# First layer of a two-layer expert lookup: u and v rows gathered as pairs, dense u and v tiles loaded as pairs

## What is computed

```python
u = jnp.take(u_tab, eid, axis=0)
act = jax.nn.gelu(jnp.einsum('chkd,cd->chk', u, hc)) * gate
v = jnp.take(v_tab, eid, axis=0)
return jnp.einsum('chk,chkd->cd', act, v)
```

## Time and profile before

| | us |
|---|---|
| runs (3): lowest, median, highest | 4078.24, 4083.88, 4086.14 |
| the profiled execution | 4085.21 |
| its span, from the first to the last instruction | 4083.4 |
| its stage with dense tiles, about | 815 to 1835 |

### The profile page before, as it was taken

The page is one execution under the profiler, slowest core; times in us unless marked ns, Lnnn a source line. Parts: engine busy times, 40 slices in busy tenths (PEclk is TensorE's granted clock), DMA queues, the critical chain, the costliest instruction groups (busy, mean ns, idle before and its releaser), DMA issues. The chain is left out here.

```text
span 4083.4 us, 41719 instructions
## 1 busy us (share of the span) xinstructions
PE 3591.4 (88%) x14914; PEld 2631.6 (64%) x14914; DVE 2362.9 (58%) x4846; ACT 649.1 (16%) x1760; POOL 889.4 (22%) x776
## 2 busy tenths in 40 slices
PE   7989987798888999988997776655999999999999
PEld 3678875687777777776784322222777676777676
DVE  2654778977788767776548887776352401352400
ACT  2531111400000000005212111101001301001300
POOL 0000000165565555540004444442000000000000
PEclk9999997999999999999999888776999999999999
DMA  4466545799999999982668999997883345683343
GB/s 173 152 178 195 148 140 204 233 392 409 409 408 369 409 409 409 408 339 90 175 186 337 417 421 383 423 422 318 277 300 112 134 155 166 222 306 114 134 155 113
DMA packets 523735, 1096.67 MB, mean 269 GB/s; under 512 B 25844, under 2 KB 339188, under 8 KB 489494
## 3 DMA queue, kind: packets, MB, share of 16 engines
q1 hardware_dynamic: 408824, 554.12, 40.0%
q0 software_dynamic: 110592, 536.92, 32.6%
q10 hardware_dynamic: 4128, 3.15, 0.3%
HBM read 1078.36 MB, written 15.73 MB: 268 GB/s over the span
## 5 line engine op out<-in xcount | busy, mean ns | idle before, releaser
L2556 PE MATMUL ps<-hT,wring 128*128 128x256 f32 x2560 | 559.7, 379 | 1.7 <-DMA wring<-in_ffn_w_up 1.7
L1676 PE MATMUL ps<-hT,wring 128*128 128x256 f32 x2048 | 485.1, 391 | 81.8 <-DVE hT L1836 79.3
L2556 PEld LDWEIGHTS ps<-hT,wring 128*128 128x128 f32 x2560 | 485.8, 190 | 85.3 <-issue 13.1
L1676 PEld LDWEIGHTS ps<-hT,wring 128*128 128x128 f32 x2048 | 388.4, 194 | 174.0 <-DVE hT L1836 120.3
L1710 POOL DMA_INDIRECT gu<-in_u_tab,eid x256 | 285.5, 1115 | 948.1 <-POOLq L134 621.4
L1667 PE MATMUL ps<-hT,wring 128*128 128x256 f32 x2048 | 464.9, 380 | 1.1 <-ACT G L1749 1.1
L1667 PEld LDWEIGHTS ps<-hT,wring 128*128 128x128 f32 x2048 | 390.5, 191 | 54.5 <-issue 1.1
L2032 PE MATMUL ps<-pairs,diag 128*128 128x512 f32 x520 | 290.2, 719 | 134.0 <-ACT diag L2127 134.0
L1860 DVE SCALAR_TENSOR_TENSOR wring<-gv,wgt,wring 128x1024 f32<-128x1024 f32 x254 | 326.6, 1286 | 109.1 <-DMA gv<-in_v_tab,eid 97.2
L1843 DVE CUSTOM_DVE_ANT_0 gu<-gu,htok 128x1024 f32<-128x1024 f32 x256 | 313.2, 1224 | 121.8 <-DMA gu<-in_u_tab,eid 116.2
L1716 POOL DMA_INDIRECT gv<-in_v_tab,eid x256 | 290.6, 1135 | 220.3 <-DVE wring L1860 154.7
(11 more groups left out here) (385 smaller groups left out, 4561.8 us busy)
## 6 DMA issues: line engine op xcount, KB each, us to landing
wring<-in_u_first SPq DMA_DIRECT2D x128, 512.0 KB
wring<-in_v_tab SPq DMA_DIRECT2D x128, 512.0 KB
room<-in_ada_w SPq DMA_DIRECT2D x32, 1536.0 KB, 11.5
wring<-in_ffn_w_gate SPq DMA_DIRECT2D x44, 1024.0 KB, 8.9
wring<-in_ffn_w_up SPq DMA_DIRECT2D x44, 1024.0 KB, 11.4
wring<-in_ffn_w_down SPq DMA_DIRECT2D x44, 1024.0 KB, 5.0
wring<-in_w_in SPq DMA_DIRECT2D x72, 512.0 KB, 6.6
wring<-in_w_mod SPq DMA_DIRECT2D x28, 1024.0 KB, 5.6
```

The costliest lines, as they stand in the source:

```text
L1676: m = nc.tensor.matmul(ps[:, n // 2, (n % 2) * S:(n % 2 + 1) * S], vslot[:, e % 2, n * P:(n + 1) * P], act_[:, e % 3, :], start=e == 0 and ...
L2556: m = mm(ps[:, b + n, q * S:(q + 1) * S], up_slot(s, q)[:, k, n * P:(n + 1) * P], hT[:, k, 0:S], start=k == 0, stop=k == KD - 1)
```

## The change

The u and v tables are laid out side by side on the host: `uv_first_rows` has rows of 8 KB, u and v of the same expert; `uv_dense[e]` has for each of 128 partitions 8 KB, the u tile e+1 (the last one: u tile 0) and the v tile e.

- **Gathers:** one gather per step fetches u and v together. There are four places for pairs (`first_pairs`, as much memory as `gu` and `gv` had), and four more in the first two quarters of `G`: two from gather 37 on, when the gates of tiles 0 to 15 have been used, and two from gather 71 on, when those of tiles 16 to 31 have. A place is free after the add.
- **Groups:** gelu and small multiply are made for two steps at a time (`LAG`), and add(n-2) follows dot(n).
- **Late gates** come back into the third and fourth quarter in turn, later than before.
- **Dense tiles:** two places, each for a u tile and a v tile. One load `load_pair(e)` brings u(e+1) and v(e) when down(e-2) is done. The u tile 0 is loaded alone ahead of them.

```diff
-                    load_v(e)
-                    if e + 2 < NE:
-                        load_u(e + 2)
-                    q, part = (e - 1) // FIRSTS - 1, (e - 1) % FIRSTS
+                    if e:
+                        load_pair(e)
+                    q, part = (e - 1) // FIRSTS - 3, (e - 1) % FIRSTS
...
+                def load_pair(e):
+                    if e == 1:
+                        sp.wait_ge(dfull.sem, 1)
                     if e >= 2:
                         sp.wait_ge(vdone.sem, e - 1)
-                    at = l * NEXP + e * NKEY
-                    sp.dma_start(vslot[:, e % 2], vb[at:at + NKEY, :]).then_inc(vtf[e % 2].sem, 16)
+                    sp.dma_start(dslot[:, e % 2], dense[e]).then_inc(densed[e % 2].sem, 16)
...
                 def up(e):
-                    pe.wait_ge(utf[e % 3].sem, 16 * (e // 3 + 1))
+                    pe.wait_ge(densed[(e + 1) % 2].sem, dense_count(e - 1))
...
+        JOIN = {steps_at(FIRSTS) + 1: (4, 5), steps_at(2 * FIRSTS) + 3: (6, 7)}
+        place, user_before, times, turn = [], [], [], deque(range(FIRST_OWN))
+        for n in range(ALL):
+            turn.extendleft(reversed(JOIN.get(n, ())))
+            r = turn.popleft()
+            turn.append(r)
+            user_before.append(max((m for m in range(n) if place[m] == r), default=None))
+            times.append(place.count(r))
+            place.append(r)
...
+                for n in range(ALL):
                     if n == COLS:
                         pool.wait_ge(routed.sem, EID1)
...
+                    if n in JOIN:
+                        pool.wait_ge(weighted.sem, FIRSTS * ((JOIN[n][0] - FIRST_OWN) // 2 + 1))
+                    if times[n]:
+                        pool.wait_ge(summed.sem, user_before[n] + 1)
+                    nc.gpsimd.indirect_dma_start(place_of(n), None, rows, bass.IndirectOffsetOnAxis(
+                        ap=eid[:, n // COLS, n % COLS:n % COLS + 1], axis=0)).then_inc(landed[place[n]].sem, 16)
...
-                        if n >= RING:
-                            add(n - RING)
-                        if n == COLS + RING:
+                        if n >= LAG:
+                            add(n - LAG)
+                        if n == COLS + 4:
```

More of the change, by code:

```diff
@@ L10 @@
 import math
+from collections import deque
 from contextlib import contextmanager
@@ L43 @@
 PAIRS, OWN = 12, 8
-RING = 4
+FIRST_OWN, FIRST_PAIRS, LAG = 4, 8, 2
 FIRSTS = 16
@@ L1536, in hybrid @@
         nc, ps, a, ident, wring = self.nc, self.ps, self.a, self.ident, self.wring
-        G, gu, gv, htok, dots, wgt = self.G, self.gu, self.gv, self.htok, self.dots, self.wgt
+        G, htok, dots, wgt = self.G, self.htok, self.dots, self.wgt
         xT, hT, mod, eid, gate, esel = self.xT, self.hT, self.mod, self.eid, self.gate, self.esel
-        ub, vb, ut = a["u_tab"], a["v_tab"], a["u_first"]
+        rows, dense = a["uv_first_rows"], a["uv_dense"]
         NE, HALF = NKEY, NKEY // 2
@@ L1561, in steps_at @@
             return min(ALL, IN_BUILD + e * (ALL - IN_BUILD) // (NE - SPARE))
-        turn_after = next(e for e in range(NE) if steps_at(e + 1) > COLS + RING - 1)
+        turn_after = next(e for e in range(NE) if steps_at(e + 1) > COLS + LAG - 1)
         L_AT, L_STEP, SUMS_AT, H_AT, TAIL_AT = 2, 2, 35, 36, 53
         EID1 = 16 * 5 + 2 + H1 * 5 + 9 + 2
-        names = [f"u{i}" for i in range(RING)] + [f"v{i}" for i in range(RING)]
+        names = [f"pair{i}" for i in range(FIRST_PAIRS)]
+        JOIN = {steps_at(FIRSTS) + 1: (4, 5), steps_at(2 * FIRSTS) + 3: (6, 7)}
@@ new lines, in hybrid, with place_of @@
+        place, user_before, times, turn = [], [], [], deque(range(FIRST_OWN))
[6 more added lines that the diff above has]
+            place.append(r)
+        def place_of(n):
+            r = place[n]
+            if r < FIRST_OWN:
+                return self.first_pairs[:, r, :]
+            at = (r - FIRST_OWN) % 2 * 2 * D
+            return G[:, (r - FIRST_OWN) // 2].rearrange("p b i t -> p (b i t)")[:, at:at + 2 * D]
@@ L1567, in hybrid, with gates_at @@
+        def gates_at(q):
+            return q if q < NQ else 2 + q % 2
         with self.phase("turned", "hready", "scored", "routed", "shifted", "exped",
-                        "m0", "m1", "rowed", "rowcopied", "colturned", "colcopied", "hot", "gfull", "gcopied", "left", "away0", "away1", "back0", "back1", "back2", "back3", "ut0", "ut1", "ut2", "vt0", "vt1", "dfull", "active", "weighted", "vdone",
+                        "m0", "m1", "rowed", "rowcopied", "colturned", "colcopied", "hot", "gfull", "gcopied", "left", "away0", "away1", "back0", "back1", "back2", "back3", "dense0", "dense1", "dfull", "active", "weighted", "vdone",
@@ L1610, in _ @@
                         sp.wait_ge(rowed.sem, HALF_UNITS)
-                        load_u(0)
-                        load_u(1)
+                        sp.dma_start(dslot[:, 1, 0:D], dense[NE - 1, :, 0:D]).then_inc(dense1.sem, 16)
+                        load_pair(0)
                 for s in range(2):
@@ L1666, in up @@
                     for k in range(KD):
-                        m = nc.tensor.matmul(ps[:, 4 + e % 2, 0:S], uslot[:, e % 3, k, :], hT[:, k, S:2 * S], start=k == 0, stop=k == KD - 1)
+                        m = nc.tensor.matmul(ps[:, 4 + e % 2, 0:S], uslot[:, (e + 1) % 2, k, :], hT[:, k, S:2 * S], start=k == 0, stop=k == KD - 1)
                     m.then_inc(dfull.sem, 1)
@@ L1673, in down @@
                     pe.wait_ge(weighted.sem, e + 1)
[L1674 removed]
+                    pe.wait_ge(densed[e % 2].sem, dense_count(e))
                     for n in range(KD):
@@ L1893, in _ @@
                     if e == NE - SPARE:
-                        for n in range(ALL - RING, ALL):
+                        for n in range(ALL - LAG, ALL):
                             add(n)
```

78 lines of the change are left out of this document (28 added, 50 removed).

## The result

| | before, us | after, us |
|---|---|---|
| runs: lowest, median, highest | 4078.24, 4082.51, 4086.14 | 4121.55, 4127.60, 4133.05 |
| the profiled execution, its span | 4085.21, 4083.4 | 4133.05, 4131.3 |

The change makes the kernel slower: ratio 1.011, 95% interval 1.0092 to 1.0129, some 45 us. The forecast was +12 (4096); the time lies 3.6 us above the upper end of its range.

What follows compares the result with a forecast made beforehand. DMA was taken to set the dense stage's pace (7.69 us a tile). Tiles to 16, 16 to 34 and 34 to 127 gave 20 - 7 + 2 = +15; less 3: +12, 4096 us, range 4058 to 4124 (own range 4084 to 4112).

Steps and rivals of the forecast that it cites:

- Larger packets: Dense stage: 8 KB rows raise DMA from 409 to 422 GB/s, 30 us less if nothing else became late.
- Four places until tile 16: First dense tiles: DVE waits for gathers; 8.4 us a tile against 7.10, +20 us (ends +6 and +42).
- the walk through two tiles: First dense tiles: step-by-step timing of gathers, dense pair and DVE, with waits of 2.4 and 0.9 us; 8.4 a tile.
- The stretch 16 to 34: Dense tiles 16 to 34: six or eight places make gathers early enough; 137.9 us against 145.1, -7.
- The pair loop, T = 7.66: Settled dense tiles: pair's issue, landing, up and down in two places give 7.66 us a tile (7.45 to 7.81), now 7.68.
- Tiles 34 to 127: Later dense tiles: DMA-paced ones -1, late gate loads +3, DVE routing work stays; sum +2 us (ends -14 and +22).
- The 3 us taken off for deep places: Dense tiles beside routing work: eight gather places spare DVE waits that four do not; 3 us off the sum.
- The groups: Dense stage, DVE: groups of two steps add 64 small multiplies of 0.2 us beside idle time; no cost.
- DMA as the bound: Rival, dense stage: places do not matter, tiles at 7.45 us; -20, 4064 us; chance 0.22.
- Slower by the pair loop and the first tiles: Rival, dense stage: queue always full at issue, 7.81 us a tile, first tiles 9.1; about +40, 4124 us; chance 0.18.
- All cancels: Rival, dense stage: first tiles at the lower end (+6), the rest as forecast (-8); 4082 us; chance 0.15.
- The dense rows do travel as 8 KB packets: Rival on dense loads said they don't: 10 of the 30 us gone, time as the forecast; no chance of its own.

Runs made afterwards that it cites:

- both_six: The changed kernel with three places for dense pairs and six early gather places, both extra ones joining at gather 7; 4054.14 us, ratio 0.9925 to the kernel before.
- halves_apart: The changed kernel, two dense places kept, with u(e+1) loaded by itself when up(e-1) is done and v(e) when down(e-2) is done; 4124.97 us.
- gathers_apart: The kernel before with dense pairs alone, in two places; u and v still gathered apart as 4 KB rows; 4083.75 us, ratio 0.9997.
- the halved pairs: The changed kernel with each dense pair loaded as two loads of 4 KB rows, same point and queue; 4219.3 us, ratio 1.0341 to the kernel before.

## Why the prediction went wrong

**Larger packets: the rate right, the gain not shown by itself.** The earlier trace rows had given 422 GB/s and 30 us, if nothing else became late. The rate came: 421 instead of 409. That both_six is 28 us below before (4082.5 to 4054.1) is near the 30 by luck in part: it has more places and its late gates elsewhere, and in the settled tiles without such loads (weighs 100 to 126) a tile takes 7.53 us, against 7.69 before and 7.45 by the rate alone.

**Four places until tile 16: right in kind, too small.** This is the step that failed first. Forecast 8.4 us a tile, measured 10.02; +20, measured +33.7 between weighs 2 and 16, and six early places take nearly all of it away (107.1). DVE's own work was right (5.76 against 5.73). What was mis-sized is the wait: the walk through two tiles gave 2.4 and 0.9 us, 1.65 a tile; the trace has 43.1 us in 128, that is 3.4 in each tile of 10.02. The 1.7 us between are the whole miss. The term behind it is the landing of a gather, "2.48 for 1.05 MB alone": with what the walk adds before it and for the dense pair, a gather was to be there 5.0 to 5.4 us after POOL's start. Measured are 7.0 in the mean of 25, some 1.8 more. Of these the last four engines make 0.9 (6.05 to 7.0); the rest is there when the first engine reports, at 5.6. In the tile shown the rows move nearly alone from 911, 1.6 us after POOL's start as the earlier trace rows had it, most engines are done by 914.95, and the dot waits for the one that ends at 917.9. I had taken the rate of full queues, which is a mean over engines, for the time of one gather on engines that run dry. The trace of before could have told: the gather of the earlier trace rows has half the bytes, 1.24 us by that rate, and its last engine reports 4.3 us after POOL's start, 2.7 us after its first row, with one more gather and some small stores beside it. I had read only its start. The upper end, 9.9, was in the text, and I put too little of the chance there: its rival was given 9.1.

**The stretch 16 to 34: wrong in sign by SP's issues, near by the weighs.** By SP's issues, as the prediction counted, 145.1 became 155.8: +11 instead of -7. By the weighs of the table it is -4.9. The two marks part because PE, and SP's issues with it, falls behind DVE there: v(16) is issued 4.2 us after weigh(14) in both kernels, v(34) 4.2 us after weigh(32) before and 14.2 after, as up waits for its pairs. Two of these tiles belong to the first term: SP issues v(e) after down(e-2), so the slow tiles up to weigh 16 reach to the issue of v(18). From v(18) to v(34) it is 129.8 before and 135.6 after, 8.48 a tile and not 7.66. "Gathers are early enough" held; what the 7.66 left out is the wait for the pair where tiles with a routing list, which are longer, take turns with tiles without: with a third place weighs 22 to 34 take 7.52 each instead of 8.02, and 7.51 with two places and u asked for earlier (halves_apart). That it is the uneven tiles which make the pair late there is my reading, and not shown.

**The pair loop, T = 7.66: near, by a reason that needs a supplement.** Up, which never waited, waits 45.2 us in about 60 tiles: 0.75 us a tile, as forecast. A tile takes 7.83 (weighs 100 to 126), 0.02 above the upper end. The 8.1 us of the pair at 1780.43 agree too. What the walk left out is the spread: from issue to the last packet a pair takes 6.0 to 9.5 us (10 to 90% of the pairs 68 to 127, by the packet records), in gathers_apart 7.1 to 8.4. A late pair holds up PE at once, and an early one gives nothing back. I had also written that half of the packets means half of the bytes; true with equal packets only. In gathers_apart the pair has two thirds of the bytes, and the same two places cost nothing against the kernel before; in after one half, and they cost 34 us against three places. That a pair of wide gathers takes share away from the dense queue was not in the prediction at all.

**Tiles 34 to 127: +2 forecast**, measured +6.5 by SP's issues (-4.0 up to 68, +10.5 from there) and +12.9 by the weighs (+6.2 and +6.7). Weighs 68 to 100, where half of the 16 loads of late gates now lie, took 7.9 to 8.1 us a tile in after and in the kernels made from it (the halved pairs apart), with two pair places or three; what a load costs there was not tried. The 3 us taken off for deep places were not to be seen.

**The groups: right.** Two steps in place of four cost 0 to 8 us in the kernel before.

**The rivals.** DMA as the bound (4064) needed pairs that land within 7.8 us; with three places and six gather places DMA is the bound, at 4054. "Slower by the pair loop and the first tiles" (4124) came nearest, 3.6 us below the time: it had T 7.81 (7.83 came) and first tiles at 9.1 (10.02). Its reason, a queue that is full at every issue of a pair, is not borne out by pairs that take anything from 6.0 to 9.5 us. I gave it 0.18, because I took the walk for a mean value when it was the best case of a chain in which whoever is last decides. "All cancels" (4082) needed the lower end of the first tiles and did not come. The dense rows do travel as 8 KB packets: 0.79 MB in 110 packets, small ones included, in the rows from 1784.

What stays open: why the first engine of an early gather needs 5.6 us, and why some end their part up to 3.6 us after the others. In 840 to 958 of after 9% of the 8 KB packets took over 500 ns (median 309), in 1500 to 1600 0.5%, in both_six's 840 to 950 0.1%: long packets go with engines that run dry, but which causes which no run here tells.

## What to carry to other kernels

Count, for each place, the chain from free to used again, with the measured landing time of a gather on engines that run dry in it, up to its slowest engine, and not the mean rate; if that chain is longer than the time that the places give, wider transfers make it worse, since each place is then held longer. When two queues share the engines, ask which of the two is waited for and look at its packets: widening those of the other queue takes share from it, and then the loads that are waited for must be asked for earlier. A change that brings two edits at once should be costed as a pair and apart: here the dense pairs alone cost nothing, the paired gathers alone 35 us, and the two were good only with a third dense place and one or two more gather places. And a total that agrees with a theory or a rival should be taken apart by stretches before it is believed: in halves_apart a gain late and a loss early cancelled.

## What the runs showed of the hardware

- Two queues that both have work get about equal numbers of packets (0.51 to 0.53 for the dense queue), not equal bytes: 110 to 110 packets and 0.88 to 0.79 MB with 8 KB each; 156 to 151 packets and 1.15 to 0.55 MB with 8 KB against 4 KB. Halving the packets of the queue that is waited for cost 92 us, with its loads asked for as late as in after.
- An early gather of 1.05 MB was there 7.0 us after POOL's start (mean of 25; 5.5 to 8.95), the first of its 16 engines 5.6 us after it. In the widest case the twelfth reported after 5.9 us and the last after 8.95. One of 0.52 MB took 4.3 us.
- The engines' time for a byte isn't fixed: 317 GB/s at a busy share of 0.88, 415 at 1.01.
